# One decoder layer with product-key experts: eight more gathered tokens, 24 places for streamed blocks, and gates normed right behind the sort

## What is computed

```python
def chunk(hc):                                    # 128 tokens at a time
    T = hc.shape[0]
    q = (hc @ wq).reshape(T, PEER_HEADS, 2, PEER_KEY_DIM)
    s1 = jnp.einsum('thd,hnd->thn', q[:, :, 0], sub_keys[:, 0])
    s2 = jnp.einsum('thd,hnd->thn', q[:, :, 1], sub_keys[:, 1])
    v1, i1 = lax.top_k(s1, PEER_TOPK)
    v2, i2 = lax.top_k(s2, PEER_TOPK)
    cand = (v1[..., :, None] + v2[..., None, :]).reshape(T, PEER_HEADS, PEER_TOPK * PEER_TOPK)
    sc, ci = lax.top_k(cand, PEER_TOPK)
    e = (jnp.take_along_axis(i1, ci // PEER_TOPK, axis=-1) * PEER_NKEYS
         + jnp.take_along_axis(i2, ci % PEER_TOPK, axis=-1))
    g = jax.nn.softmax(sc, axis=-1)
    act = jax.nn.gelu(jnp.einsum('td,thkd->thk', hc, exp_u[e]), approximate=False)
    return jnp.einsum('thk,thkd->td', (g * act).astype(hc.dtype), exp_v[e])
```

## Time and profile before

| what | us |
|---|---|
| median of 3 runs | 838.3 |
| lowest, highest | 837.05, 839.43 |
| the profiled execution, whole time | 837.85 |
| the profiled execution, span | 835.8 |

### The profile page before, as it was taken

One profiled execution on the slowest core, in us unless ns is written; L12 is line 12 of the kernel. 1 busy time (PEld: TensorE's weight loads), 2 busy tenths in 40 slices (PEclk: granted clock), 3 DMA queues, 4 the chain that ended last, 5 costly groups with the idle time before them and its releaser, 6 DMA issues.

```text
span 835.8 us, 14512 instructions
## 1 busy us (share of the span) xinstructions
PE 798.2 (96%) x5726; PEld 754.5 (90%) x5726; DVE 571.7 (68%) x1146; ACT 169.5 (20%) x444; POOL 237.3 (28%) x224
## 2 busy tenths in 40 slices
PE   6999999899999999599999999999999999999996
PEld 4988879889999888599999999988889999999996
DVE  4959879698997999378888988755543444443422
ACT  4464475552111112012111111100000000000003
POOL 2000000000003545254543444733333234334300
PEclk9999999999999999899999999999999999999998
DMA  9998882653878999999999999999999999999981
GB/s 339 405 369 332 350 351 104 243 199 138 274 241 328 410 408 409 307 373 409 408 408 409 405 398 372 411 409 408 409 409 409 408 405 409 408 407 408 408 332 52
DMA packets 77215, 294.30 MB, mean 352 GB/s; under 512 B 8799, under 2 KB 11103, under 8 KB 75868
## 3 DMA queue, kind: packets, MB, share of 16 engines
q1 hardware_dynamic: 49148, 192.15, 59.6%
q0 software_dynamic: 28000, 101.23, 30.9%
HBM read 291.25 MB, written 1.56 MB: 350 GB/s over the span
## 4 chain that ended last, share of the span: by engine, by line
PE 65%; DMA 27%; DVE 5%; issue 1%; ACT 1%; another core or an unknown queue 0%; SPq 0%; ACTq 0%; DVEq 0%; POOLq 0%
PE banks L1213 24%; PE banks L1242 22%; DMA raw<-in_v_b 13%; DMA raw<-in_u_t 10%; PE banks L958 3%; PE banks L1225 2%; PE banks L876 2%; PE banks L911 2%; PE banks L954 2%; DMA raw<-in_w_mod 2%; DMA rows<-in_u_rows,idx 1%; PE banks L1027 1%; PE banks L881 1%; DVE sc_w L1352 1%; PE banks L927 1%
## 5 line engine op out<-in xcount | busy, mean ns | idle before, releaser
L1213 PE MATMUL banks<-hT,raw 128*128 128x160 f32 x2048 | 293.0, 302 | 11.8 <-DMA raw<-in_u_t 8.7
L1213 PEld LDWEIGHTS banks<-hT,raw 128*128 128x128 f32 x2048 | 282.0, 191 | 18.5 <-DMA raw<-in_u_t 18.0
L1242 PE MATMUL banks<-act,raw 128*128 128x160 f32 x2048 | 293.2, 302 | 5.0 <-DMA raw<-in_v_b 0.8
L1242 PEld LDWEIGHTS banks<-act,raw 128*128 128x128 f32 x2048 | 280.0, 190 | 17.2 <-DMA raw<-in_v_b 16.0
L1720 DVE SCALAR_TENSOR_TENSOR row_sums<-rows,weight,row_sums 128x1024 f32<-128x1024 f32 x94 | 120.7, 1284 | 147.5 <-DMA rows<-in_v_b,idx 146.0
L558 POOL DMA_INDIRECT rows<-in_u_rows,idx x96 | 119.8, 1248 | 169.9 <-DVE dots L1697 84.6
L558 POOL DMA_INDIRECT rows<-in_v_b,idx x96 | 109.5, 1141 | 166.0 <-PE banks L1242 110.2
L1697 DVE CUSTOM_DVE_ANT_0 rows<-rows,h_rows 128x1024 f32<-128x1024 f32 x96 | 115.0, 1220 | 26.5 <-DMA rows<-in_u_rows,idx 26.0
L808 ACT ACTIVATE turned<-banks,ccol 128x256 f32<-128x256 f32 x8 | 3.8, 472 | 289.3 <-PE banks L1242 289.3
L766 ACT ACTIVATE act<-banks 128x160 f32<-128x160 f32 (+19 forms) x123 | 33.0, 270 | 139.7 <-PE banks L1213 135.2
L539 POOL DMA_DIRECT2D h_lines<-h_stage x1 | 0.5, 522 | 204.5 <-ACT h_stage L791 204.5
(11 more groups left out here) (235 smaller groups left out, 792.7 us busy)
## 6 DMA issues: line engine op xcount, KB each, us to landing
raw<-in_u_t SPq DMA_DIRECT2D x128, 512.0 KB
raw<-in_v_b SPq DMA_DIRECT2D x128, 512.0 KB
wq<-in_wq SPq DMA_DIRECT2D x2, 4096.0 KB, 18.1
sh_w<-in_w_mod SPq DMA_DIRECT2D x8, 512.0 KB, 13.1
sc_w<-in_w_mod SPq DMA_DIRECT2D x8, 512.0 KB, 13.4
win<-in_w_in SPq DMA_DIRECT2D x8, 512.0 KB, 14.1
win<-in_w_in SPq DMA_DIRECT2D x1, 4096.0 KB, 20.9
sc_w<-in_w_mod SPq DMA_DIRECT2D x2, 2048.0 KB, 23.5
```

The costliest lines, as they stand in the source:

```text
L1213: last = nc.tensor.matmul(dst, raw[n % RAW][:, c * P:(c + 1) * P], hT[:, c, 0:MANY], start=(c == 0), stop=(c == DC - 1))
L1242: return nc.tensor.matmul(chunk_place(c)[:, 0:MANY], raw[(BLOCKS + j) % RAW][:, c * P:(c + 1) * P], act[:, j, :], start=(j == 0 and c < 4) ...
```

## The change

The gathered tokens become 104 in kinds of 64, 32 and 8, the dense ones 152. There are so 104 gathers a table, 208 in all, and 19 groups of gates instead of 20. The new kind has its own load of h2 rows: 8 lines of DRAM, each read 16 times.

The blocks' buffers are listed as `SPOTS`, places with the last block number that may lie in each. The first six are those of before, to the end of the stream. 18 more lie in memory that is free for a while: places of the query weights, of the keys and scores, and two that are kept to the end. The list has 24 entries. A block takes the place whose last user is oldest among those still open to it. Worked out from the list, a block waits for the use of the block 24 before it for blocks 24 to 38, 22 for blocks 39 to 55 (19 for 56 and 57), 12 for blocks 58 to 75, and 8 from block 76 to the end; before it was 6 everywhere. So block 57 is let go by block 38, and block 58 by block 46.

The list of chosen experts and the first kind's rows are now issued by ScalarE, between its own instructions for the blocks: out behind block 22's GELU, in behind block 24's. The rows of the two later kinds come behind blocks 64 and 67 in SyncE's loop.

`EARLY` is 28, and the line `some_dots(EARLY - dotted[0])` behind the sort is gone; three dots stand ahead of the copy of the turned gates. `TURN_AT` is 63, `GATE_AT` 68, `PACE_U` 0.85 and `PACE` 1.26: the last gather (k = 103) is let go at block 128 + 117 = 245.

```diff
-RAW = 6
-KINDS = (64, 32)
+KINDS = (64, 32, 8)
-EARLY = 32
+EARLY = 28
-H2_FIRST = (9, 11)
-H2_LATER = (58,)
-EXPERTS_OUT = 25
-EXPERTS_IN = 26
-EXP_AT = 52
+ROWS_AT = 48
+H2_LATER = (64, 67)
+EXPERTS_OUT = 23
+EXPERTS_IN = 25
+EXP_AT = 55
-TURN_AT = 60
-GATE_AT = 65
+TURN_AT = 63
+GATE_AT = 68
-PACE = 1.36
-PACE_U = 1.0
-BEFORE_TURN = 2
+PACE = 1.26
+PACE_U = 0.85
+BEFORE_TURN = 3
...
-        raw_word = [RAW0, RAW0 + D, R[4], R[4] + D, R[4] + 3 * D, G20]
-        raw = [at(f"raw{n}", raw_word[n], [P, D]) for n in range(RAW)]
+        LASTING = [RAW0, RAW0 + D, R[4], R[4] + D, R[4] + 3 * D, G20]
+        AFTER_WQ0 = [(16384 + n * D, GATE_AT) for n in range(4)] + [(22528, ROWS_AT - 1), (23552, ROWS_AT - 1), (8192, 8192 // MANY)]
+        AFTER_HIGH = [(R[3], STREAM), (R[3] + D, STREAM)]
+        AFTER_WQ1 = [(4096 + n * D, (4096 + n * D) // MANY) for n in range(4)] + [(M0, EXP_AT - 1), (M0 + D, EXP_AT - 1)]
+        AFTER_SCORES = [(M0 + 2 * D, EXP_AT - 1), (M0 + 3 * D, EXP_AT - 1), (R[3] + 7 * D, EXP_AT - 1)]
+        SPOTS = [(w, STREAM) for w in LASTING] + AFTER_WQ0 + AFTER_HIGH + AFTER_WQ1 + AFTER_SCORES
+        raw = [at(f"raw{n}", w, [P, D]) for n, (w, until) in enumerate(SPOTS)]
...
+        spot_of, user_before, fills = [], [], []
+        for n in range(STREAM):
+            users = [max([m for m in range(n) if spot_of[m] == s], default=s - len(SPOTS))
+                     for s in range(len(SPOTS))]
+            s = min((s for s in range(len(SPOTS)) if SPOTS[s][1] >= n), key=lambda s: users[s])
+            spot_of.append(s)
+            user_before.append(users[s])
...
+                if n == len(LASTING):
+                    sp.wait_ge(group_done, WQ + 4)
+                if n == SPOTS.index(AFTER_HIGH[0]):
+                    sp.wait_ge(group_done, WQ + 6)
+                if n == SPOTS.index(AFTER_WQ1[0]):
+                    sp.wait_ge(group_done, WQ + 8)
+                if n == SPOTS.index(AFTER_SCORES[0]):
+                    sp.wait_ge(s_ready, TT * LISTS // 4)
+                if user_before[n] >= 0:
+                    sp.wait_ge(block_used, user_before[n] + 1)
...
                     sp.wait_ge(h2_saved, 16)
+                    sp.wait_ge(block_used, ROWS_AT)
...
+                if n == EXPERTS_OUT:
+                    sc.wait_ge(chosen_ready, 1)
+                    sc.dma_start(expert_lines.ap(), e_u[FEW0:P, :]).then_inc(idx_in, 16)
+                if n == EXPERTS_IN:
+                    sc.wait_ge(idx_in, 16 + 16)
+                    for kind in range(len(KINDS)):
+                        sc.dma_start(idx[:, KIND_AT[kind]:KIND_AT[kind + 1]], lines_of(expert_lines, kind)
+                                     ).then_inc(idx_in, 16)
...
-            some_dots(EARLY - dotted[0])
             ve.wait_ge(gate_exp, TT)
```

37 lines of the change are left out of this document (14 added, 23 removed).

## The result

| what | us |
|---|---|
| the changed kernel, median of 4 runs (lowest, highest) | 853.26 (851.15, 854.0) |
| the kernel before, 4 runs beside it (lowest, highest) | 838.87 (837.05, 839.49) |
| changed / before, with its 95% interval | 1.0176 (1.015 to 1.0202) |
| profiled execution of the changed kernel, whole time and span | 854.0, 852.2 |
| predicted | 845.0 (830 to 857) |

The changed kernel is 14.4 us slower by the medians, where +7 was forecast: the sign is right, the size is half.

What follows compares the result with a forecast made beforehand. DMA, full at about 408 GB/s from 302 us on, was taken to bound the kernel. Items 1 to 6 gave +7.9 us and the end -0.9, so +7 on 837.85, about 845 us (range 830 to 857).

Steps and rivals of the forecast that it cites:

- item 4: Slow reads of repeated lines: the 32-line read costs the same as before, the new 8-line read adds +1.9 us.
- item 3: Gathers by 302 us: the first goes about 4.4 us later, 1.5 tiles less, +1.9 us, 2.6 at most.
- item 5: From 350 to 356 us: the DMA loss with nothing in flight on GpSimd and SyncE goes, -1.3 us.
- TensorE's part: Blocks of 152 columns take 2.08 us, saving 25 us of TensorE's time, costed at nothing except behind the last gather.
- Item 1: Bytes moved from 302 us on: 16 more gathers, +20.6 us, and one more load of h2 rows, +1.3.
- Item 2: Blocks landed by 302 us: 58 in, 14 tiles ahead of before, -18.0 us.
- "much slower" rival: The 8-line read is far worse than the 32-line one, costing 8 to 15 us of DMA: 852 to 860, chance 0.16.
- Items 5 and 6: Item 5 as above; item 6, the gate stage, where DMA is not quite filled: +1.5 us, 0 to 4.
- The norm of the gates: Right behind the sort, done at 337.5 us; TensorE waits about 2 us; costed at nothing beyond item 5.
- The end: After the last gather (block 245): blocks at TensorE's 2.08 us, `few_sums` +1.8, together -0.9 us.
- The faster one: Rival: deeper buffers keep DMA at 408 GB/s, so losses go, -6.4 us, 832; chance 0.22.
- The level case: Rival: items 3 and 4 cost nothing and the gate stage keeps 398 GB/s: 838 to 840, chance 0.2.

Runs made afterwards that it cites:

- e2: The kernel before with the 104 gathered tokens alone (kinds 64, 32, 8, PACE 1.26), six buffers kept: 861.49 us, ratio 1.0279.
- e9: The kernel before with the repeated rows of the kind of 32 made by TensorE and ScalarE, not read from DRAM: 833.73 us, ratio 0.9946.
- e11: The changed kernel with both repeated reads replaced by TensorE's product, the expert list moved by SyncE, `few_sums` two blocks later: 837.9 us, ratio 0.9998.
- e6: The changed kernel with the list of experts written out and read in by SyncE instead of ScalarE: 848.7 us, ratio 1.014.
- e4: The kernel before with four 512 KB loads added in product 2, of 128, 32, 8 and one different lines: 854.17 us, ratio 1.019.
- e3: The changed kernel with 96 gathered tokens (kinds 64 and 32, one late load of rows), PACE still 1.26: 838.2 us, ratio 1.0006.
- e8: The changed kernel with the move of the norm of the gates alone undone (`EARLY` 32, two dots ahead of the copy): 856.4 us, ratio 1.0227.
- e5: The changed kernel with `few_sums` ahead of the last two blocks instead of the last four: 848.24 us, ratio 1.0138.

## Why the prediction came out half right

**The step that failed** is the sum's size, in its losses and not in its bytes: DMA from 302 us on was +14.9 us where items 1 to 6 gave +7.9, and the end was +1.5 for -0.9. Three terms were too small: the two reads in item 4 (+1.9 forecast, +4.4 measured), the late first gathers in item 3 (+1.9, with a bound of 2.6, for 3.9), and `few_sums` at the end (+1.8, for 6.0 with its wait and the fallen clock). One term was missing and so stood at nothing: the 2.4 us that DMA isn't full from 302 to 322 us. And the move of the norm, costed at nothing beyond item 5, was worth some 6 us ahead of the end.

**What bounds the kernel** was right, and carried all that followed. TensorE was busy 11 us less and the kernel became slower; e2's 23.4 us are 17 tiles and a slow read; e9 took 10 us of waiting and slow work from TensorE and 4.5 were gained.

**TensorE's part** was right: 2.06 us for a block, forecast 2.08.

**Item 1**, the bytes, was right (+22.0 for +21.9).

**Item 2**, blocks ahead at 302 us, was right: 58 are in, and 43 were before, by the trace's landings. That is 15, not 14. But the item ended its look at 302 us. Up to 322 us the places open one by one behind TensorE's blocks, and DMA moves 359 GB/s, a loss of 2.4 us that no term had. It is no price of the reads: in e11, which has none, the same 20 us run at 345.

**Item 3**, the first gathers, failed in size. ScalarE's read of the list was issued at 257.09, as worked out (256.8). But from the end of the issues to the first gather it took 264.82 - 258.99 = 5.8 us, where the prediction carried over the 2.6 us of SyncE's read before. In e6, on SyncE again but beside a fuller stream, it took 258.33 - 254.68 = 3.65. So of the 8.2 us the later issue is about half. Three gathers fewer at 302 us (16 for 19) are 3.9 us; I had 1.9 with a bound of 2.6, and the bound didn't hold it either. That ScalarE's queue is the cause of the longer way isn't shown: over seven kernels each it took 4.5 to 7.0 us with ScalarE and 2.5 to 4.5 with SyncE, the last in e11.

**Item 4**, the slow read, was right for the read alone (1.8 in e4, forecast 1.9) and wrong for the changed kernel. The two reads were costed one by one, 3.9 and 1.9. They are issued 6 us apart and run into each other: 18 us at 240 GB/s and some more behind, 8.3 together. e3, with one read in the same kernel, loses 4.0 between 326 and 340 (292 GB/s), so the second adds 4.3 here. That the meeting is what makes it dear isn't shown. In e2 the same two reads are issued 7.5 us apart and meet as well (219 GB/s from 340 to 350 us), yet from 334 to 366 us DMA lost (408 - 311) / 408 * 32 = 7.6 us there and (408 - 321) / 408 * 32 = 6.8 in the kernel before. One thing that differs is GpSimd's queue: in these two kernels it moved 2 and 0 packets of 4 KB from 344 to 350 us, in the changed kernel 478 in its slow stretch from 322 to 340. The item also put its two loads on one scale, the number of lines; by their landings the load of 32 lines differs from both others in a second way (e4). That the time fell into the band of the "much slower" rival is no point for that rival. It needed 8 to 15 us for the read of 8 lines, and e4 and e3 give 1.8 and 4.3.

**Items 5 and 6** were right within half a microsecond. Item 5's reason was read wrongly: the last parts of blocks 60 to 64, which had been issued by 343.54, landed only from 352.2 to 360.2, so SyncE's queue was not empty from 350 to 356 us.

**The norm of the gates** came at 346.1, not 337.5: VectorE's first tile was 8 us late, and in the slow stretch it waited for tiles again. TensorE stood 10.09 us, not 2. That this costs next to nothing was the boldest step, and e8 tests it: 14.5 us more of standing cost 6 us by the start of `few_sums` and 3 to 4 in the whole time. Most of the wait is hidden behind DMA, as forecast, and zero was too low.

**The end** failed in sign. I had -0.9 and the rest of the account is +1.5. The pace of blocks behind the last gather was thought to be TensorE's 2.08; it stayed at 2.56 for six blocks more, since the gathers issued last still shared the engines: GpSimd's queue moves as many packets as SyncE's until 818 us. And `few_sums` was +1.8 in the sum, while its own 3.4, the wait of 1.01 and the 1.6 of the matmuls behind are +6.0; e5 gets 3.2 of that back. I took one row's duration (3.65 for 32) and scaled it. The row says nothing of a wait in front of it, nor of a clock below full behind that.

**The sum.** Of the 9.4 us between forecast and profiled execution, 1.6 are the head start, 2.5 the reads, 2.4 the stretch behind the head start, 0.5 small terms and 2.4 the end. All have one sign. Each term was costed for itself, and nothing was set aside for the places where the new things meet: late gathers and a full stream, a gather queue and the last blocks, two reads. That this is the common cause is my reading; the runs show the terms.

**The rivals.** The faster one, in which deeper buffers keep DMA at 408, is refuted by the 240 GB/s with a share of 1.03: buffers don't mend a slow transfer. Its other half has something: with 96 tokens the places win 4.6 us. The level case, 838 to 840, needed items 3 and 4 to cost nothing, and they cost 3.9 and 4.4. Of the signs named, the 58 blocks and the emptier DMA before 302 us came (259 GB/s from 290 to 302); the norm, the start of product 2 (512.42 for 505) and the last gather (806.45 for 803) came later than named.

What stays open is why reads of few lines are slow. In the changed kernel the median 4 KB packet takes 0.16 us from 527 to 796 us and 0.27 to 0.28 us from 322 to 340, on GpSimd's queue as on SyncE's. So it is not the one queue that is held up but everything that is read then. Why, no run shows. The four completions of the read of 32 lines would account for how long its slow stretch lasts and for the late quarter of the blocks behind it, but not for slower packets on both queues, which the read of 8 lines with its 16 completions shows as well.
